# A new order of the expert products on TensorE, with gathers issued further ahead and gate weights freed by their own semaphore

## The chip, the cores and the metric

The kernel runs on one core of one Trainium2 chip. The metric is the device time of one execution in microseconds (us), the median of several runs. The profile is one execution of its own, taken by the hardware profiler; its times within the program are counted from the start of the span.

## The reference, cut to what matters

One layer of an encoder runs over 576 tokens (512 of a prompt, 64 of a running stream): a projection, two state-space mixers, cross-attention, and a mixture of experts at the end. The change lies in the last part alone. Each token picks one group of experts and two experts in it; the sum runs over 32 experts.

```python
for e in range(N_EXPERTS):          # 32 experts, d_model 1024, hidden width 256
    hid = silu(t @ w_gate[e]) * (t @ w_up[e])
    out = out + (hid @ w_down[e]) * combine[:, e:e + 1]
```

Each of w_gate, w_up and w_down of one expert has 1024 x 256 float32 numbers, 1 MB. All 32 experts together are 96 MB of weights that are read from HBM once.

## The kernel before, in words

The kernel is written engine by engine, with every wait on a semaphore by hand. There is no scheduler: the order on each engine is the order of the code.

**Routing.** After the attention a table of slots gives each expert up to 80 tokens (CAP). The normed token rows lie in HBM (`ffn_rows`); results go to `expert_rows` in HBM and are mixed at the very end, after all experts.

**One expert n on TensorE (PE).** Four steps, each with its own line: `turn_x` (L1385) transposes the gathered rows `xg` in 8 small matmuls (all transposes carry the helper's line L907); `gate_up` (L1393) makes the gate product and then the up product, 32 matmuls each (all carry L1407, and the trace records them as 64); `down_rows` (L1411) makes the down product in 24 matmuls (L1423, recorded as 48). In the loop of `pe_pass` (L1429) the order is: transposes of n, down product of n-1, gate product of n, up product of n.

**The other compute engines.** ScalarE (ACT) copies half of the transposed rows to `xgT` (L1758), applies silu to the gate product (L1763) and copies part of the down product to `yo` (L1771, L1772). VectorE (DVE) copies the other half (L2306), multiplies silu(gate) by up into `hid` (recorded at the helper's line L1816) and copies the rest of the down product (L2319, L2320). All of these have two buffers, one for even and one for odd experts.

**Weights.** There are five sets of three weight buffers (gate, up, down; `WSET`). The loads of experts 0 to 4, 15 transfers, are issued before the expert stage, as buffers of earlier stages come free. From then on `reload` (L678) on SyncE (SP) fills a buffer again when it is free, one transfer of 1 MB (L675) each, always in the order gate, up, down: expert 31 into the set of expert 0, then expert 5 into the set of expert 1, and so on to expert 30 into that of expert 26. The waits stand in this order on the one SP queue:

```python
if part < 2:
    sp.wait_ge(gu_done, N + 1)        # gate and up: up product of the old expert done
else:
    sp.wait_ge(dn_done, 2 * N + 2)    # down: its down product done
load_part(BODY * i + n, set_of(n), part)
```

So SP asks for no gate weights of the next expert before the down weights of this one have been asked for.

**Rows.** GpSimd (POOL) gathers the rows of an expert from `ffn_rows` into one of two `xg` buffers (`gather`, L840, issued at L851) and scatters `yo` to `expert_rows` (`scatter`, L856, issued at L866), both as indirect DMAs. In `pool_pass` (L871) it issues the gather of expert n+2 and then the scatter of expert n.

**After the experts.** When all scatters have landed SP loads `expert_rows` (L728) and the final norm follows. In between SP issues one load of the final norm's gain (L591), right behind the last weights.

Of the kernel before, what the change touches and what calls it, by code (L numbers as in the profile page):

```python
# [216 lines left out]
def build(nc, a, o):  # L217
# [14 lines left out]
    with ExitStack() as ctx:  # L232
# [346 lines left out]
        def _(sp):  # L579
# [162 lines left out]
        def _(pool):  # L742
# [97 lines left out]
            def gather(pp, i, b, reused=True):  # L840

                if reused:
                    pool.wait_ge(turned_x, 4 * pp + (2 * b - 2))
                    pool.sem_inc(waits_done, 1)
                    pool.tensor_copy(cur_x[0:CAP, b:b + 1], idx_x[0:CAP, bass.ds(2 * i + b, 1)]).then_inc(gx_copied, 1)  # L845
                    pool.wait_ge(gx_copied, 2 * pp + (b - 1))
                    pool.sem_inc(waits_done, 1)
                    rows_now = cur_x[0:CAP, b:b + 1]
                else:
                    rows_now = idx_x[0:CAP, b:b + 1]  # L850
# [5 lines left out]
            def scatter(pp, i, b, reused=True):  # L856

                if reused:
                    pool.wait_ge(scattered[b], 16 * pp)
                    pool.sem_inc(waits_done, 1)  # L860
                pool.tensor_copy(cur_y[0:CAP, b:b + 1], idx_y[0:CAP, bass.ds(2 * i + b, 1)]).then_inc(gy_copied, 1)
                pool.wait_ge(gy_copied, 2 * pp + (b + 1))
                pool.wait_ge(yo_act, 2 * pp + (b + 2))
                pool.wait_ge(yo_dve, 2 * pp + (b + 2))
                pool.sem_inc(waits_done, 1)
                pool.indirect_dma_start(  # L866
                    out=y2_dram[:, :], out_offset=bass.IndirectOffsetOnAxis(ap=cur_y[0:CAP, b:b + 1], axis=0),
                    in_=yo[b][0:CAP], in_offset=None,
                    bounds_check=2 * T - 1, oob_is_err=False).then_inc(scattered[b], 16)

            def pool_pass(p):  # L871
                first = p * (LAST + 1)
# [12 lines left out]
                for b in range(2):  # L885
                    scatter(first + LAST, LAST, b)
                for b in range(2):
                    pool.wait_ge(scattered[b], 16 * (first + LAST + 1))
                pool.sem_inc(pass_done, 1)
# [6 lines left out]
        def _(pe):  # L896
# [488 lines left out]
            def turn_x(pp, b):  # L1385

                pe.wait_ge(gathered[b], 16 * pp + 16)
# [5 lines left out]
            def gate_up(N, n, i, p, reused=True):  # L1393

                s, b = set_of(n), n % 2
                gate, up = [w.rearrange("p (k n) -> p k n", k=KD) for w in WSET[s][0:2]]
# [4 lines left out]
                for part, (w, done) in enumerate(((gate, gate_done), (up, gu_done))):  # L1401
                    wait_expert_chunk(pe, part, n, i, p)
                    for j in range(2):
                        for k in range(KD):
                            for half in range(2):
                                cols = slice(HD * half, HD * (half + 1))
                                m = pe.matmul(banks[2 + part][cols, CAP * j:CAP * (j + 1)], w[:, k, j::2][:, cols],  # L1407
                                              xgT[b][:, k, :], start=(k == 0), stop=(k == KD - 1))
                    m.then_inc(done, 1)
# [19 lines left out]
            def pe_pass(p):  # L1429
# [14 lines left out]
                turns = (NE - 4) // BODY  # L1444
                with pe.Fori(0, turns) as i:
# [29 lines left out]
        def _(act):  # L1475
# [279 lines left out]
            def copy_x(pp, b):  # L1755

                act.wait_ge(turned_x, 4 * pp + (2 * b + 1))
# [3 lines left out]
            def act_expert(pp, b, last=False, reused=True):  # L1761
                act.wait_ge(gate_done, 2 * pp + (b + 1))
                act.activation(gact[b].rearrange("p j l -> p (j l)"), banks[2][:, 0:2 * CAP], ACT.Silu)\  # L1763
                    .then_inc(silu_done, 1)
                if not last:
                    copy_x(pp + b, 1 - b)
                act.wait_ge(dn_done, 4 * pp + (2 * b + 1))
                if reused:
                    act.wait_ge(scattered[b], 16 * pp)
# [4 lines left out]
            def act_pass(p):  # L1774
                first = p * (LAST + 1)
                again = not isinstance(p, int)
                copy_x(first, 0)
                for b in range(2):
                    act_expert(first, b, reused=again)
                with act.Fori(1, LAST) as i:  # L1780
                    for b in range(2):
                        act_expert(first + i, b)
                for b in range(2):
                    act_expert(first + LAST, b, last=(b == 1))
# [15 lines left out]
        def _(dve):  # L1800
# [502 lines left out]
            def copy_x(pp, b):  # L2303

                dve.wait_ge(turned_x, 4 * pp + (2 * b + 2))
# [3 lines left out]
            def dve_expert(pp, b, last=False, reused=True):  # L2309
                dve.wait_ge(silu_done, 2 * pp + (b + 1))  # L2310
                dve.wait_ge(gu_done, 2 * pp + (b + 1))
                tt(hid[b].rearrange("p j l -> p (j l)"), gact[b].rearrange("p j l -> p (j l)"),
                   banks[3][:, 0:2 * CAP]).then_inc(hid_ready, 1)
                if not last:
                    copy_x(pp + b, 1 - b)
                dve.wait_ge(dn_done, 4 * pp + (2 * b + 2))
                if reused:
                    dve.wait_ge(scattered[b], 16 * pp)
# [25 lines left out]
            def dve_pass(p):  # L2344
# [24 lines left out]
                copy_x(first, 0)  # L2369
                for b in range(2):  # L2370
                    dve_expert(first, b, reused=again)
                with dve.Fori(1, LAST) as i:
                    for b in range(2):
                        dve_expert(first + i, b)
                for b in range(2):
                    dve_expert(first + LAST, b, last=(b == 1))
# [55 lines left out]
```

## Time and profile before

| what | value |
|---|---|
| runs before | 908.38, 908.22, 906.3 us; median 908.22 us |
| the profiled execution's own time | 909.06 us |
| its span in the profile | 907.3 us, so 1.76 us lie around it |
| mean granted TensorE clock | 0.966 of full speed |
| TensorE busy, share of the span | 91% (weight loads 75%) |
| VectorE, ScalarE, GpSimd busy | 39%, 23%, 15% |
| bytes moved by DMA | 167.61 MB, mean 185 GB/s |
| the expert stage, first transposes to last down product | 581.7 to 869.0 us of the span |

A busy TensorE in this profile is not a TensorE at its peak, since matmuls are pipelined. In the views, PE is TensorE's matmuls, PEld its weight loads. "DMA share" is the mean busy share of the core's 16 DMA engines, and every wait on a transfer counts 16 arrivals. An entry in brackets at the end of a row of the timeline is the idle time of that engine before the row and what ended it.

### The profile page before, as it was taken

The page shows a single profiled execution, that of the slowest core. Times are in us where ns is not written, and L with a number is a line of the kernel's source. Part 1 is how long each engine was busy: PE and PEld are TensorE (multiplying, and loading weights), DVE is VectorE, ACT ScalarE, POOL GpSimd, SP SyncE. Part 2 cuts the span into 40 slices and gives each one's busy share as a digit, 9 for nine tenths or more (in the row PEclk, how much of TensorE's full clock was granted, in tenths as well). Part 3 has the DMA queues.
Part 4 walks back from the last instruction along what each step waited for, and adds up shares of the span by engine and source line. Part 5 has one row for each costly group of instructions (what it writes and reads, how often), then busy time and mean ns, then how long its engine had stood idle before and what let it go on. Part 6 is the DMA issues. An engine that isn't in the chain of part 4 may idle for free. (4 is left out here: it accounts for less than half of the span.)

```text
span 907.3 us, 21592 instructions
## 1 busy us (share of the span) xinstructions
PE 829.5 (91%) x9261; PEld 682.2 (75%) x9261; DVE 350.1 (39%) x791; ACT 211.5 (23%) x484; POOL 136.1 (15%) x173
## 2 busy tenths in 40 slices
PE   3999999899999999999999998699999999998925
PEld 2777877677888888877888886578788788777722
DVE  5599987425551123401223447411211211111216
ACT  2302206425221201112221212122222222221203
POOL 1191100004420000000000000123232232222100
PEclk9999999989999999999999998599999999999977
DMA  9742174102121850151022324589999999999335
GB/s 239 230 112 42 21 173 139 47 12 96 47 94 70 292 184 1 61 172 47 1 92 71 135 98 183 232 317 374 376 373 383 372 394 371 382 363 331 127 113 224
DMA packets 76535, 167.61 MB, mean 185 GB/s; under 512 B 25712, under 2 KB 56560, under 8 KB 63616
## 3 DMA queue, kind: packets, MB, share of 16 engines
q1 hardware_dynamic: 61060, 151.45, 46.8%
q0 software_dynamic: 6144, 9.45, 3.1%
q10 hardware_dynamic: 9276, 5.93, 2.2%
q8 instruction: 40, 0.66, 0.3%
q14 instruction: 15, 0.12, 0.0%
HBM read 158.09 MB, written 17.88 MB: 194 GB/s over the span
## 5 line engine op out<-in xcount | busy, mean ns | idle before, releaser
L940 PE MATMUL bank<-act_a,weight_ring 128*128 128x288 f32 x768 | 192.2, 412 | 3.4 <-ACT act_a L1487 1.8
L940 PEld LDWEIGHTS bank<-act_a,weight_ring 128*128 128x128 f32 x768 | 146.9, 193 | 44.5 <-ACT act_a L1487 2.4
L1229 PE MATMUL bank<-weight_ring,act_b 128*128 128x256 f32 x512 | 111.8, 379 | 0.0
L1229 PEld LDWEIGHTS bank<-weight_ring,act_b 128*128 128x128 f32 x512 | 96.7, 190 | 12.9
L1816 DVE TENSOR_TENSOR region_t<-region_t,bank 128x160 f32<-128x160 f32 (+3 forms) x47 | 15.5, 331 | 147.6 <-PE bank L1407 147.1
L1407 PE MATMUL bank<-region_t,weight_ring 128*64 128x80 f32 x1536 | 58.4, 235 | 4.7 <-DMA weight_ring<-in_w_up 4.0
L1407 PEld LDWEIGHTS bank<-region_t,weight_ring 128*64 128x64 f32 x1536 | 55.8, 140 | 8.6 <-DMA weight_ring<-in_w_up 4.6
L866 POOL DMA_INDIRECT expert_rows<-region_r,scatter_now x32 | 30.1, 941 | 191.0 <-DVE region_r L2320 191.0
L1130 PE MATMUL bank<-weight_ring,region_u 128*128 128x256 f32 x256 | 56.6, 380 | 0.0
L1130 PEld LDWEIGHTS bank<-weight_ring,region_u 128*128 128x128 f32 x256 | 48.4, 190 | 6.5
L1816 DVE TENSOR_TENSOR region_u<-region_u,bank 128x512 f32<-128x512 f32 (+1 forms) x26 | 17.8, 686 | 90.2 <-PE bank L1229 66.1
L1487 ACT ACTIVATE act_a<-bank 128x512 f32<-128x512 f32 (+1 forms) x46 | 22.5, 523 | 118.2 <-PE bank L907 91.1
L907 PE MATMUL bank<-ident,region_r 80*128 80x80 f32 (+1 forms) x324 | 45.0, 282 | 3.8 <-DMA region_r<-ffn_rows,gather_index 3.8
L907 PEld LDWEIGHTS bank<-ident,region_r 80*128 80x128 f32 (+1 forms) x324 | 39.0, 191 | 8.1 <-issue 3.9
L2319 DVE COPY region_r<-bank 16x256 f32<-16x256 f32 x32 | 13.7, 429 | 78.3 <-PE bank L1423 78.3
L834 POOL MEMSET region_r<- 80x1024 f32 x2 | 1.8, 948 | 262.4 <-PE bank L1298 262.4
L1407 PEld LDWEIGHTS bank<-region_t,region_g 128*64 128x64 f32 x1024 | 36.8, 138 | 5.2 <-issue 3.0
L1407 PE MATMUL bank<-region_t,region_g 128*64 128x80 f32 x1024 | 39.0, 234 | 1.5 <-DMA region_g<-in_w_up 1.5
L1771 ACT ACTIVATE region_r<-bank 32x256 f32<-32x256 f32 x64 | 24.2, 378 | 67.3 <-PE bank L1423 66.9
L907 PE MATMUL bank<-ident,row_stage 128*128 128x128 f32 (+2 forms) x141 | 20.4, 295 | 18.9 <-DVE row_stage L1834 17.0
L907 PEld LDWEIGHTS bank<-ident,row_stage 128*128 128x128 f32 (+2 forms) x141 | 17.1, 158 | 22.1 <-issue 18.4
L851 POOL DMA_INDIRECT region_r<-ffn_rows,gather_now x30 | 29.3, 976 | 25.9 <-POOL gather_now L845 14.7
(341 smaller groups left out, 1146.5 us busy)
## 6 DMA issues: line engine op xcount, KB each, us to landing
weight_ring<-in_w_up SPq DMA_DIRECT2D x17, 1024.0 KB
weight_ring<-in_w_down SPq DMA_DIRECT2D x10, 1024.0 KB, 6.3
weight_ring<-in_w_in SPq DMA_DIRECT2D x8, 1024.0 KB, 7.6
region_g<-in_w_up SPq DMA_DIRECT2D x8, 1024.0 KB
region_g<-in_w_gate SPq DMA_DIRECT2D x8, 1024.0 KB
conv_io<-in_w_gate SPq DMA_DIRECT2D x8, 1024.0 KB
conv_io<-in_w_down SPq DMA_DIRECT2D x8, 1024.0 KB
weight_ring<-in_w_gate SPq DMA_DIRECT2D x7, 1024.0 KB
```

The costliest lines, as they stand in the source:

```text
L834: pool.memset(xg[b][0:CAP], 0.0).then_inc(xg_zero, 1)
L851: pool.indirect_dma_start(out=xg[b][0:CAP], out_offset=None, in_=xf_dram[:, :], in_offset=bass.IndirectOffsetOnAxis(ap=rows_now, axis=0), ...
L866: pool.indirect_dma_start(out=y2_dram[:, :], out_offset=bass.IndirectOffsetOnAxis(ap=cur_y[0:CAP, b:b + 1], axis=0), in_=yo[b][0:CAP], in_ ...
L907: return pe.transpose(out, in_, ident[0:m, 0:m])
L940: m = pe.matmul(ps[:, 0:HALF], slot(c)[:, k, P * (mt % 2):P * (mt % 2 + 1)], x[:, k, HALF * h:HALF * (h + 1)], start=(k == 0), stop=(k == ...
L1130: m = pe.matmul(ps[:, 0:CW], mnT[:, k, P * t:P * (t + 1)], slot(first_chunk + c)[:, k, :], start=(k == 0), stop=(k == KD - 1))
L1229: m = pe.matmul(ps[0:L, CW * cc:CW * (cc + 1)], x[:, k, t0:t0 + L], slot(c)[:, k, :], start=(k == 0), stop=(k == KD - 1))
L1407: m = pe.matmul(banks[2 + part][cols, CAP * j:CAP * (j + 1)], w[:, k, j::2][:, cols], xgT[b][:, k, :], start=(k == 0), stop=(k == KD - 1))
L1487: act.activation(dst, src, func, scale=scale).then_inc(emptied["act"], 1)
L1771: act.activation(yo[b][DB * blk:DB * (blk + 1), 3 * CW:D], down_block(b, blk, 3), ACT.Copy)
L1816: return dve.tensor_tensor(out, x, y, op)
L2319: dve.tensor_copy(yo[b][DB * 2:CAP, 3 * CW:D], down_block(b, 2, 3))
```

## The change

TensorE's order per expert becomes: gate product of n, transposes of n+1, down product of n-1, up product of n. `gate_up` is split into `gate` and `up` over one helper `hidden`. The gate product now waits for the silu of the expert before (`silu_done`) where `gate_up` waited for its `hid_ready`. On SP the load into a gate buffer waits for `gate_done` instead of `gu_done`; the order gate, up, down on the queue stays. On POOL the first four gathers are issued ahead of everything else as their buffers come free, and then gather n+4 stands before scatter n; there are still two `xg` buffers, so gather N waits until expert N-2 has been transposed, as before. ACT and DVE follow the new order. Counts of instructions, transfers and bytes stay the same.

```diff
                 for part in range(3):
-                    if part < 2:
+                    if part == 0:
+                        sp.wait_ge(gate_done, N + 1)
+                    elif part == 1:
                         sp.wait_ge(gu_done, N + 1)
                     else:
                         sp.wait_ge(dn_done, 2 * N + 2)
...
-            def gather(pp, i, b, reused=True):
+            def gather(n, i, p, reused=True):
+                b, N = n % 2, NE * p + 2 * i + n
                 if reused:
-                    pool.wait_ge(turned_x, 4 * pp + (2 * b - 2))
+                    pool.wait_ge(turned_x, 2 * (N - 1))
...
+                for n in range(4):
+                    gather(n, 0, p, reused=n >= 2)
+                for n in range(2):
+                    gather(n + 4, 0, p)
+                    scatter(n, 0, p, reused=again)
+                with pool.Fori(0, (NE - 6) // 2) as i:
+                    for n in range(2, 4):
+                        gather(n + 4, i, p)
+                        scatter(n, i, p)
+                for n in range(NE - 4, NE):
+                    scatter(n, 0, p)
                 for b in range(2):
-                    gather(first, 0, b, reused=again)
-                for b in range(2):
-                    gather(first + 1, 1, b)
-                    scatter(first, 0, b, reused=again)
-                with pool.Fori(1, LAST) as i:
-                    for b in range(2):
-                        gather(first + i + 1, i + 1, b)
-                        scatter(first + i, i, b)
...
+            def gate(N, n, i, p, reused=True):
                 pe.wait_ge(xT_act, N + 1)
                 pe.wait_ge(xT_dve, N + 1)
                 if reused:
-                    pe.wait_ge(hid_ready, N)
+                    pe.wait_ge(silu_done, N)
+                hidden(0, gate_done, n, i, p)
+            def up(n, i, p):
+                hidden(1, gu_done, n, i, p)
...
-                turn_x(N0 // 2 if not again else p * (NE // 2), 0)
-                gate_up(N0, 0, 0, p, reused=again)
-                turn_x(p * (NE // 2), 1)
+                turn_x(0, 0, p)
+                gate(N0, 0, 0, p, reused=again)
+                turn_x(1, 0, p)
+                up(0, 0, p)
+                gate(N0 + 1, 1, 0, p)
+                turn_x(2, 0, p)
                 down_rows(N0, 0, 0, p, reused=again)
-                gate_up(N0 + 1, 1, 0, p)
+                up(1, 0, p)
...
                     for n in range(2, 2 + BODY):
-                        turn_x(p * (NE // 2) + i * (BODY // 2) + n // 2, n % 2)
+                        gate(N0 + i * BODY + n, n, i, p)
+                        turn_x(n + 1, i, p)
                         if n == 2:
                             down_rows(N0 + i * BODY + 1, BODY + 1, i - 1, p)
                         else:
                             down_rows(N0 + i * BODY + (n - 1), n - 1, i, p)
-                        gate_up(N0 + i * BODY + n, n, i, p)
+                        up(n, i, p)
                 for n in range(NE - 2, NE):
-                    turn_x(p * (NE // 2) + n // 2, n % 2)
+                    gate(N0 + n, n, 0, p)
+                    if n < NE - 1:
+                        turn_x(n + 1, 0, p)
                     down_rows(N0 + n - 1, n - 1, 0, p)
-                    gate_up(N0 + n, n, 0, p)
+                    up(n, 0, p)
                 down_rows(N0 + NE - 1, NE - 1, 0, p)
...
                 with act.Fori(0, (NE - 4) // 2) as i:
                     for n in range(3, 5):
                         act_gate(n, i, p)
                         copy_x(n + 1, i, p)
                         act_rows(n - 1, i, p)
...
                 with dve.Fori(0, (NE - 4) // 2) as i:
                     for n in range(3, 5):
                         copy_x(n + 1, i, p)
                         dve_rows(n - 1, i, p)
                         dve_hidden(n, i, p)
```

## Rows read from the trace of the kernel before

**Rows 1.** Page, part 2: DMA share in 40 slices of the span.

```profile
DMA  9742174102121850151022324589999999999335
```

**Rows 2.** Waits of TensorE's matmuls, 560 to 870 us: total us, times, longest.

```profile
PE bank L1407 <- DMA weight_ring<-in_w_up: 4.0, 4, 1.3
PE bank L907 <- DMA region_r<-ffn_rows,gather_index: 3.8, 1, 3.8
...
PE bank L1423 <- DVE region_t L1816: 2.8, 7, 0.5
PE bank L1407 <- DMA act_a<-in_w_up: 1.8, 2, 1.2
PE bank L1407 <- DMA region_g<-in_w_up: 1.5, 2, 1.0
```

**Rows 3.** Timeline of TensorE, one expert in the middle (start us, us, instructions).

```profile
694.89 1.11 PE L907 MATMUL bank<-ident,region_r 80*128 80x80 f32 x8
695.93 2.80 PE L1423 MATMUL bank<-act_a,region_t 128*32 128x256 f32 x48
698.66 2.44 PE L1407 MATMUL bank<-region_t,conv_io 128*64 128x80 f32 x64
700.93 2.44 PE L1407 MATMUL bank<-region_t,region_g 128*64 128x80 f32 x64
```

**Rows 4.** Timeline of TensorE, first and last wait for up weights, and the end.

```profile
788.41 2.44 PE L1407 MATMUL bank<-region_t,weight_ring 128*64 128x80 f32 x64 [1.27 <-DMA weight_ring<-in_w_up]
...
854.90 2.44 PE L1407 MATMUL bank<-region_t,weight_ring 128*64 128x80 f32 x64 [0.53 <-DMA weight_ring<-in_w_up]
857.27 1.11 PE L907 MATMUL bank<-ident,region_r 80*128 80x80 f32 x8
858.31 2.80 PE L1423 MATMUL bank<-weight_ring,region_t 128*32 128x256 f32 x48
861.04 2.44 PE L1407 MATMUL bank<-region_t 128*64 128x80 f32 x64
863.31 2.38 PE L1407 MATMUL bank<-region_t,weight_ring 128*64 128x80 f32 x64
866.18 2.80 PE L1423 MATMUL bank<-weight_ring,region_t 128*32 128x256 f32 x48 [0.49 <-DVE region_t L1816]
```

**Rows 5.** Windows: us, busy PE PEld DVE ACT POOL, granted clock, DMA share, GB/s.

```profile
580.00:590.00 10.00, 7.65 (x116) 7.47 (x118) 1.27 (x3) 2.02 (x3) 2.36 (x4) 0.54 0.07 20
590.00:600.00 10.00, 10.00 (x218) 8.43 (x214) 1.66 (x4) 2.09 (x5) 2.32 (x4) 1.00 0.80 302
...
620.00:780.00 160.00, 157.76 (x3450) 130.59 (x3440) 30.64 (x74) 39.32 (x94) 42.80 (x74) 1.00 1.00 380
...
830.00:860.00 30.00, 27.71 (x586) 21.90 (x589) 5.48 (x13) 6.50 (x16) 5.76 (x10) 1.00 0.49 179
```

**Rows 6.** Page, part 6: the load behind the last weights, us from issue to landing.

```profile
gain_rows<-in_norm_final SPq DMA_DIRECT2D x1, 512.0 KB, 32.2
```

**Rows 7.** Timeline of all engines, the first expert, with SP's issues.

```profile
583.65 4.54 PE L1407 MATMUL bank<-region_t 128*64 128x80 f32 x64 [0.63 <-ACT region_t L1758]
...
587.94 2.97 PE L1407 MATMUL bank<-region_t,weight_ring 128*64 128x80 f32 x64
...
590.84 1.11 PE L907 MATMUL bank<-ident,region_r 80*128 80x80 f32 x8
590.93 0.33 SPq L675 DMA_DIRECT2D region_t<-in_w_gate  x1
...
591.31 0.43 SPq L675 DMA_DIRECT2D weight_ring<-in_w_up  x1
...
594.74 0.33 SPq L675 DMA_DIRECT2D weight_ring<-in_w_down  x1
...
600.14 0.35 SPq L675 DMA_DIRECT2D conv_io<-in_w_gate  x1
```

**Rows 8.** Page, part 3: GpSimd's queue of gathers and scatters, share of 16 engines.

```profile
q0 software_dynamic: 6144, 9.45, 3.1%
```

More of the change, by code:

```diff
@@ L849, in gather @@
                 else:
-                    rows_now = idx_x[0:CAP, b:b + 1]
+                    rows_now = idx_x[0:CAP, n:n + 1]
                 pool.indirect_dma_start(
@@ L854, in gather, with scatter @@
                     bounds_check=T - 1, oob_is_err=False).then_inc(gathered[b], 16)
-            def scatter(pp, i, b, reused=True):
+            def scatter(n, i, p, reused=True):
+                b, N = n % 2, NE * p + 2 * i + n
                 if reused:
-                    pool.wait_ge(scattered[b], 16 * pp)
+                    pool.wait_ge(scattered[b], 16 * (NE // 2) * p + 16 * i + 16 * (n // 2))
                     pool.sem_inc(waits_done, 1)
[L861 to L864, printed above, removed]
+                pool.tensor_copy(cur_y[0:CAP, b:b + 1], idx_y[0:CAP, bass.ds(2 * i + n, 1)]).then_inc(gy_copied, 1)
+                pool.wait_ge(gy_copied, N + 1)
+                pool.wait_ge(yo_act, N + 2)
+                pool.wait_ge(yo_dve, N + 2)
                 pool.sem_inc(waits_done, 1)
@@ L871, in pool_pass @@
             def pool_pass(p):
-                first = p * (LAST + 1)
                 again = not isinstance(p, int)
@@ L875, in pool_pass @@
                 pool.sem_inc(waits_done, 1)
-                for b in range(2):
-                    gather(first, 0, b, reused=again)
-                for b in range(2):
-                    gather(first + 1, 1, b)
-                    scatter(first, 0, b, reused=again)
-                with pool.Fori(1, LAST) as i:
-                    for b in range(2):
-                        gather(first + i + 1, i + 1, b)
-                        scatter(first + i, i, b)
[L885 to L888, printed above, removed]
+                for n in range(4):
[9 more added lines that the diff above has]
+                    scatter(n, 0, p)
+                for b in range(2):
+                    pool.wait_ge(scattered[b], 16 * (NE // 2) * p + 16 * (NE // 2))
                 pool.sem_inc(pass_done, 1)
@@ L1383, in _, with turn_x @@
                 pe.wait_ge(emptied[who], count[who])
-            def turn_x(pp, b):
-                pe.wait_ge(gathered[b], 16 * pp + 16)
+            def turn_x(n, i, p):
+                b = n % 2
+                pe.wait_ge(gathered[b], 16 * (NE // 2) * p + 16 * (BODY // 2) * i + 16 * (n // 2 + 1))
                 for h in range(2):
@@ L1391, in turn_x, with hidden @@
                     m.then_inc(turned_x, 1)
-            def gate_up(N, n, i, p, reused=True):
+            def hidden(part, done, n, i, p):
                 s, b = set_of(n), n % 2
-                gate, up = [w.rearrange("p (k n) -> p k n", k=KD) for w in WSET[s][0:2]]
+                w = WSET[s][part].rearrange("p (k n) -> p k n", k=KD)
+                wait_expert_chunk(pe, part, n, i, p)
+                for j in range(2):
+                    for k in range(KD):
+                        for half in range(2):
+                            cols = slice(HD * half, HD * (half + 1))
+                            m = pe.matmul(banks[2 + part][cols, CAP * j:CAP * (j + 1)], w[:, k, j::2][:, cols],
+                                          xgT[b][:, k, :], start=(k == 0), stop=(k == KD - 1))
+                m.then_inc(done, 1)
+            def gate(N, n, i, p, reused=True):
                 pe.wait_ge(xT_act, N + 1)
@@ L1399, in gate_up @@
                 if reused:
-                    pe.wait_ge(hid_ready, N)
[L1401 to L1409, printed above, removed]
+                    pe.wait_ge(silu_done, N)
+                hidden(0, gate_done, n, i, p)
+            def up(n, i, p):
+                hidden(1, gu_done, n, i, p)
             def down_rows(N, n, i, p, reused=True):
@@ L1438, in pe_pass @@
                 pe.wait_ge(idx_ready, p + 1)
[L1439 to L1441 removed]
+                turn_x(0, 0, p)
[4 more added lines that the diff above has]
+                turn_x(2, 0, p)
                 down_rows(N0, 0, 0, p, reused=again)
[L1443 to L1445 removed]
+                up(1, 0, p)
+                with pe.Fori(0, (NE - 4) // BODY) as i:
                     for n in range(2, 2 + BODY):
[L1447 removed]
+                        gate(N0 + i * BODY + n, n, i, p)
+                        turn_x(n + 1, i, p)
                         if n == 2:
@@ L1774, in act_pass @@
             def act_pass(p):
-                first = p * (LAST + 1)
                 again = not isinstance(p, int)
[L1777 to L1784, printed above, removed]
+                copy_x(0, 0, p)
+                act_gate(0, 0, p)
+                copy_x(1, 0, p)
+                for n in range(1, 3):
+                    act_gate(n, 0, p)
+                    copy_x(n + 1, 0, p)
+                    act_rows(n - 1, 0, p, reused=again)
+                with act.Fori(0, (NE - 4) // 2) as i:
+                    for n in range(3, 5):
+                        act_gate(n, i, p)
+                        copy_x(n + 1, i, p)
+                        act_rows(n - 1, i, p)
+                act_gate(NE - 1, 0, p)
+                act_rows(NE - 2, 0, p)
+                act_rows(NE - 1, 0, p)
             act.sem_inc(yo_act, 1)
@@ L2368, in dve_pass @@
                     expert_gates()
[L2369 to L2376, printed above, removed]
+                copy_x(0, 0, p)
+                copy_x(1, 0, p)
+                dve_hidden(0, 0, p)
+                for n in range(1, 3):
+                    copy_x(n + 1, 0, p)
+                    dve_rows(n - 1, 0, p, reused=again)
+                    dve_hidden(n, 0, p)
+                with dve.Fori(0, (NE - 4) // 2) as i:
+                    for n in range(3, 5):
+                        copy_x(n + 1, i, p)
+                        dve_rows(n - 1, i, p)
+                        dve_hidden(n, i, p)
+                dve_rows(NE - 2, 0, p)
+                dve_hidden(NE - 1, 0, p)
+                dve_rows(NE - 1, 0, p)
             dve.sem_inc(yo_dve, 1)
```

42 lines of the change are left out of this document (23 added, 19 removed).

## The prediction

> **What bounds the kernel now.** I read the DMA line of the page first, because the change touches only the expert stage and that stage moves 96 MB of weights. From about two thirds of the span on, the 16 DMA engines are 90% busy or more for ten slices of 22.7 us each [rows 1]. The reader is to see that this is the expert stage, and that it begins with a hole: from 580 to 590 us the share is 0.07, then 0.80, and from 620 to 780 us it is 1.00 at 380 GB/s [rows 5].
>
> Next I read what TensorE waits for. In a middle expert its steps follow one another without a gap: transposes 1.04 us (695.93 less 694.89), down product 2.73, gate product 2.27 [rows 3], up product 2.37 (857.27 less 854.90) [rows 4]. That is 8.41 us of work per expert. Its waits on the way are small: 2.8 us for VectorE's `hid`, and 4.0 + 1.8 + 1.5 = 7.3 us for up weights; for gathered rows it waits once, 3.8 us before expert 0 [rows 2]. Taken alone this would say that TensorE is the bound.
>
> The last two views say otherwise. The waits for up weights are eight, one per expert, and all late: the first such up product starts at 788.41 us, the last at 854.90 [rows 4]: 66.49 / 7 = 9.50 us per expert, 1.1 us more than PE's work. So in the end PE follows the transfers, one per 9.50 / 3 = 3.17 us. And not all DMA engines are equal: from 830 to 860 us the mean share is only 0.49 [rows 5], while PE is still waiting for up weights at 854.90 [rows 4] and the gain's load right behind the last weights takes 32.2 us to land [rows 6]. Some engines have long finished and a few have not; a transfer counts when its last part is there. **The bound is the slowest DMA engine**, which works through 81 transfers from SP's first issue at 590.93 us [rows 7] to the end: to 854.90 it has done 80 of them, (854.90 - 590.93) / 80 = 3.30 us each, close to the 3.17 at which PE visibly waits for it. There is no room for much idle time in between. So the end of the stage is: when this engine starts, plus its fixed work, plus what PE must still do after the last weights.
>
> **The change, part by part.**
>
> *Volume.* 81 transfers, 32 gathers, 32 scatters before and after: 0.
>
> *PE's steadier order.* The gaps for `hid` (2.8 us in all [rows 2]) go, since a gate product and transposes now lie between the up product and the down product that needs `hid`. With 8.41 us per expert against 9.50 PE only waits longer for weights: 0 on the path. The copies and products on ACT and DVE change places too; with ACT busy 39.32 and DVE 30.64 of 160 us [rows 5] they are hidden, and if that cover went, a late `xgT` copy would hold the next gate product.
>
> *The start.* Gate product 0 ends where the up product starts, at 587.94 us; up ends at 590.84 and SP issues 0.09 later [rows 7]. The first transfer (expert 31's gate) moves from 590.93 to 588.03, **2.90 us earlier**. But then SP stands at its second and third wait, and these come later in PE's new order. After gate 0 come transposes of 1 (to 589.1, a little long at the low clock), up 0 (2.37, to 591.5), gate 1 (2.27), transposes of 2 (1.04), down 0 (2.73, to 597.5). So the up transfer is issued at 591.6 instead of 591.31 and the down transfer at 597.6 instead of 594.74 [rows 7]; expert 5's gate load, free since 593.8, stands behind that down wait on SP and goes out with it, instead of at 600.14. Before, three transfers from 590.93 at 3.17 us last to 600.4, just when the fourth is issued at 600.14 [rows 7]: no gap. After, the third starts at 597.6 and ends at 600.8, the fourth ends at 603.9 against 603.6 before: 0.3 us later. In the new gap, however, the engine does the rows of one more gather, since POOL no longer issues gathers behind a scatter. All gathers and scatters take 3.1% of 16 engines' span [rows 8], 28.1 us per engine, 0.44 us per transfer spread evenly, 0.88 if half of the engines carry it. Bounds of the term: -2.9 (the whole lead is kept) to +0.4. I take +0.3 - 0.88 = **-0.6 us**, with the uneven value, because the engines visibly end unevenly [rows 5, 6].
>
> *Later releases.* In every later round the down weights are asked for 2.27 us later and the gate weights 2.37 us earlier than before, as seen from the up product. The queue of the slowest engine is never empty then (1.1 us of arrears are added per expert), and its order is still gate, up, down: 0. If the arrears were not there, each round would lose up to 2.3 us.
>
> *Gathers.* POOL's wait for transposes n+2 now stands ahead of scatter n. These transposes come before down product n on PE, so the scatter queued behind that wait is not delayed by it. A gather still has two experts' time to land, and PE never waits for one in the stage's course [rows 2]: 0.
>
> *The tail.* This is the part that I expect to cost. Before, PE waits for the last up weights; from the start of up 30 at 854.90 to the start of the last down product at 866.18 are 11.28 us [rows 4]: up, transposes, down, gate, up and 0.49 of wait. After, PE meets expert 30's gate weights first. They land one transfer before the up weights, and behind them stand gate 30 (2.27), transposes 31 (1.04), down 29 (2.73), up 30 (2.37), gate 31 (2.27), down 30 (2.73), up 31 (2.38), wait (0.49): 16.28 us. From the landing of the up weights that is 16.28 - 3.17 = 13.11, so **+1.8 us**. The up and down weights of 30 land meanwhile. Bounds: 0, if PE no longer has to wait at gate 30, to 16.28 - 2.76 - 11.28 = +2.2, with a transfer spacing of 1.05 MB at the middle stretch's 380 GB/s [rows 5]. PE is ready for gate 30 only some 8.4 us after it began gate 29, against 9.5 between landings, so I take the value near the upper end.
>
> *Sum.* -0.6 + 1.8 = +1.2 us on the profiled execution's own 909.06 us (span 907.3 and 1.76 around it), 910.3 us. That execution lies 0.84 us above the median of the runs, 908.22; the same step from the median gives **909.4 us**. The bounds add up to -2.9 and +2.6, or 905.3 to 910.8. Before's three runs spread over 2.1 us; a change under 0.3% (2.7 us) can't be told from none.
>
> **The rivals.**
>
> *A. The earlier first transfer is kept.* The slowest engine would then do useful work from 588.03 on without a gap and everything ends 2.9 us earlier; with the tail, -2.9 + 1.8 = -1.1, 907.1 us. For it: the hole from 580 to 590 us [rows 5]. Against it: SP's order on the queue. The Trainium skill, "DMA: Bandwidth & Descriptors", section "Rules for kernel authors", advises to issue a DMA early, compute, and wait late. By that rule this lead is the gain; the trace of before shows only that the first transfer waits for the up product.
>
> *B. PE becomes the pace.* If the weights keep up with 8.41 us per expert, the wait for up weights is gone and gate 31 starts at 591.5 + 30 x 8.41 = 843.8; then 2.27 + 2.73 + 2.38 + 0.49 bring the last down product to 851.7 instead of 866.18: -14.5, 893.7 us, or half of it if only part of the waits goes. For it: PE's 157.76 busy of 160 us in the middle [rows 5]. Against it: 9.50 us per expert as soon as the early stock of weights is used up [rows 4].
>
> *C. TensorE's clock rises later.* It was granted 0.54 of full speed from 580 to 590 us and 1.00 from 590 to 600 [rows 5]; before it rose, PE ran gate 0 and the beginning of up 0. The new order puts eight short transposes into that place. If the low level (1.2 instead of 2.4 GHz) lasts until up 0 has ended, up 0 costs what gate 0 did, 4.29 us instead of 2.27 [rows 7, 4], some 2.0 more, and with it every release behind it, at a moment at which the DMA engines are idle: +1.2 + 2.0 = +3.2, 911.4 us, slower. It decides from the point at which the clock has not risen by 591.5 us. For it: the transposes have short streams. Against it: they follow without a gap. The skill's "TensorE: Matmul & The Clock Gate", section "What's actually happening", says that the number of slow matmuls at the start differs between runs of one kernel; no run here shows that.
>
> *D. The change doesn't do what it says.* "Gate weights first" holds for one transfer alone; from then on the gate load stands behind the down wait. This is part of the forecast, not a case of its own.
>
> **How the numbers follow.** The forecast, 909.4 us, gets 0.58; of that 0.15 lies above +2.7 us, by the upper bounds and the runs' spread. A gets 0.10 (no change that can be told), B 0.17 (faster), C 0.12 (slower), anything else 0.03 (slower). Faster by over 0.3%: 0.17. Within 0.3%: 0.43 + 0.10 = 0.53. Slower: 0.15 + 0.12 + 0.03 = 0.30. The range goes from the forecast's lower bound, 905.3, rounded to 905.0, to beyond C, 912.0; B and the 0.03 are left out.
>
> **What would show it.** Right: the first SP issue of the stage at 588, the third near 597.6 with the fourth right behind it; PE's waits for up weights gone and as large or larger ones for gate weights from about the same expert on, 9.5 us apart; the last wait of this kind about three microseconds before 854.9; the last down product near 867. Wrong: no waits for weights at all and the last down product before 860 (B); a first transfer followed by a busy DMA share and the last down product before 866 (A); a granted clock that rises only after 591.5 us (C); or waits for gathers on PE.

## The result, and the profile after

The changed kernel takes **914.25 us** (median of 10 executions, 909.44 to 918.74), the kernel before, run beside it, 907.92: ratio **1.0063, 95% interval 1.0037 to 1.0089**. It is slower by over 0.3%, and above the forecast range of 905.0 to 912.0. The profiled execution (span 907.7, own time 909.44) is the fastest of its ten, so its trace shows what the change does to the waits, but not the whole loss.

What PE waits for, from 560 to 880 us (columns as in [rows 2]):

```profile
PE bank L1406 <- DMA region_g<-in_w_gate: 4.2, 3, 2.8
...
PE bank L910 <- DMA region_r<-ffn_rows,gather_index: 3.9, 1, 3.9
PE bank L1406 <- DMA act_b<-in_w_gate: 3.7, 2, 2.1
PE bank L1406 <- DMA weight_ring<-in_w_gate: 3.7, 3, 2.7
...
PE bank L1406 <- DMA conv_io<-in_w_gate: 1.3, 2, 1.1
...
PE bank L1434 <- DVE region_t L1843: 0.5, 1, 0.5
```

As forecast, the waits for up weights are gone and waits for gate weights stand in their place. There are ten, 12.9 us in all, against eight of 7.3 us before, and they begin sooner: the first at 742.93 us, against 788.41 for the first up product that waited [rows 4]. The waits for `hid` fell from 2.8 to 0.5 us, and that bought nothing, because PE now arrives earlier at weights that come no earlier. PE's timeline, the first wait, the two longest, the last one and the end, against [rows 4]:

```profile
742.93 2.44 PE L1406 MATMUL bank<-region_t,weight_ring 128*64 128x80 f32 x64 [0.30 <-DMA weight_ring<-in_w_gate]
...
782.85 4.00 PE L1406 MATMUL bank<-region_t,weight_ring 128*64 128x80 f32 x64 [2.68 <-DMA weight_ring<-in_w_gate]
...
812.63 2.44 PE L1406 MATMUL bank<-region_t,region_g 128*64 128x80 f32 x64 [2.82 <-DMA region_g<-in_w_gate]
...
851.26 2.44 PE L1406 MATMUL bank<-region_t,region_g 128*64 128x80 f32 x64 [0.44 <-DMA region_g<-in_w_gate]
...
867.64 2.80 PE L1434 MATMUL bank<-weight_ring,region_t 128*32 128x256 f32 x48 [0.49 <-DVE region_t L1843]
```

The last down product starts at 867.64, forecast "near 867". The reader is also to see the second row: that gate product took 4.00 us instead of 2.44. From 783.5 to 786.9 us the granted clock was 0.50, the 1.2 GHz level, right after 2.68 us of waiting. SP's queue in the first rounds, against [rows 7]:

```profile
588.08 0.33 SPq L675 DMA_DIRECT2D region_t<-in_w_gate  x1
591.61 0.33 SPq L675 DMA_DIRECT2D weight_ring<-in_w_up  x1
597.62 0.33 SPq L675 DMA_DIRECT2D weight_ring<-in_w_down  x1
598.32 0.35 SPq L675 DMA_DIRECT2D conv_io<-in_w_gate  x1
599.96 0.34 SPq L675 DMA_DIRECT2D region_g<-in_w_up  x1
605.97 0.33 SPq L675 DMA_DIRECT2D conv_io<-in_w_down  x1
```

The first load goes out 2.85 us earlier than in [rows 7], the third 2.88 us later: SP stands 6.0 us at the wait for the down product. Then three loads go out within 2.3 us (597.62 to 599.96), and again nothing for 6.0. The windows (columns as in [rows 5]):

```profile
580.00:590.00 10.00, 7.80 (x104) 7.36 (x106) 1.50 (x3) 2.46 (x4) 2.08 (x4) 0.55 0.16 37
590.00:600.00 10.00, 10.00 (x238) 8.52 (x236) 1.66 (x4) 2.09 (x5) 2.83 (x5) 1.00 0.70 251
620.00:780.00 160.00, 156.78 (x3424) 127.75 (x3416) 31.18 (x75) 38.94 (x93) 42.99 (x76) 1.00 1.01 382
780.00:830.00 50.00, 43.76 (x916) 35.79 (x914) 8.31 (x20) 10.45 (x25) 11.20 (x20) 0.97 0.97 354
830.00:860.00 30.00, 26.42 (x578) 21.53 (x576) 5.03 (x13) 6.26 (x15) 5.19 (x9) 1.00 0.46 169
```

What the DMA engines gain before 590 us (share 0.16 for 0.07) they lose from 590 to 600 (0.70 for 0.80). From 830 to 860 the mean share is 0.46 while PE still waits at 851.26: so the load that PE waits for still ends later than most of the engines' work.

### The profile page after: what moved, and what is told of

It reads as the page before. It is cut to its first block and busy times, and to the rows that moved or that the text cites. A ratio compares the mean times of both kernels' runs of the same rounds, so it can differ in the third digit from the quotient of the medians.

```text
span 907.7 us, 21617 instructions
## 1 busy us (share of the span) xinstructions
PE 828.4 (91%) x9261; PEld 680.7 (75%) x9261; DVE 350.2 (39%) x791; ACT 211.3 (23%) x484; POOL 135.6 (15%) x173
## 2 busy tenths in 40 slices
DMA packets 76535, 167.61 MB, mean 185 GB/s; under 512 B 25712, under 2 KB 56560, under 8 KB 63616
## 5 line engine op out<-in xcount | busy, mean ns | idle before, releaser
L1232 PEld LDWEIGHTS bank<-weight_ring,act_b 128*128 128x128 f32 x512 | 96.8, 190 | 12.9
L2334 DVE COPY region_t<-bank 128x320 f32<-128x320 f32 x32 | 15.7, 491 | 111.6 <-PE bank L910 111.6
L1782 ACT ACTIVATE region_t<-bank 128x160 f32<-128x160 f32 x32 | 9.7, 303 | 146.6 <-PE bank L1406 146.6
```

The costliest lines, as they stand in the source:

```text
L1232: m = pe.matmul(ps[0:L, CW * cc:CW * (cc + 1)], x[:, k, t0:t0 + L], slot(c)[:, k, :], start=(k == 0), stop=(k == KD - 1))
```

## The experiments

Theory: the slowest DMA engines set the pace, and the change costs because SP's queue (gate, up, down) no longer has the order in which PE uses the weights (gate of n+1, down of n, up of n+1). Rivals: the early gate load itself costs (e2, e10, e13, e14), or the clock that falls behind long waits (e6, e9). The expectations call this last one "theory 2" in e1 to e6 and "theory C" in e9 and e11; it is not rival C of the prediction, which was about the start of the stage. The table gives all seventeen runs. "Stage" is worked out from the trace: start of the last down product less start of the first transposes.

| run | kernel | median us | ratio, 95% | stage us |
|---|---|---|---|---|
| | before, first trace | 907.92 | | 284.46 |
| e5 | before again, one execution | 903.93 | | 281.04 |
| | changed, first trace | 914.25 | 1.0063, 1.0037 to 1.0089 | 286.07 |
| e1 | changed again | 913.15 | 1.0045, 1.0023 to 1.0068 | 285.28 |
| e11 | changed, third time | 913.17 | 1.0060, 1.0037 to 1.0083 | 286.84 |
| e2 | changed, gate freed with up | 910.87 | 1.0022, 0.9999 to 1.0044 | 287.07 |
| e10 | the same again | 910.89 | 1.0027, 1.0004 to 1.0050 | 284.16 |
| e13 | changed, only first gate load early | 910.68 | 1.0032, 1.0012 to 1.0052 | 282.68 |
| e14 | changed, only later gate loads early | 916.45 | 1.0100, 1.0078 to 1.0121 | 287.09 |
| e6 | changed, eight spare products | 921.13 | 1.0143, 1.0119 to 1.0167 | 294.95 |
| e9 | changed, three spare products | 912.52 | 1.0054, 1.0032 to 1.0076 | 285.19 |
| e3 | changed, loads in order of use | 905.73 | 0.9952, 0.9934 to 0.9971 | 277.78 |
| e15 | the same, three loads together | 904.71 | 0.9968, 0.9951 to 0.9986 | 279.23 |
| e4 | before, gate freed first | 904.68 | 0.9951, 0.9933 to 0.9969 | 276.93 |
| e7 | before, rows spread | 896.91 | 0.9873, 0.9850 to 0.9896 | 269.98 |
| e8 | changed, rows spread | 893.92 | 0.9853, 0.9825 to 0.9882 | 268.42 |
| e12 | order of use, rows spread | 896.04 | 0.9866, 0.9841 to 0.9891 | 269.26 |
| e16 | before, gate freed first, rows spread | 896.35 | 0.9872, 0.9848 to 0.9896 | 269.65 |
| e17 | changed, gate freed with up, rows spread | 897.41 | 0.9852, 0.9827 to 0.9878 | 269.65 |

The runs of before beside them had medians of 907.3 to 910.2 us.

### How far single executions differ (e1, e5, e11)

No edit.

> The changed kernel once more, unchanged. Its ten runs lie between 909.44 and 918.74 us (median 914.25), the profiled one is the fastest of them. Theory 1 (order of use): gate weights are needed before the down weights but are loaded behind them, so TensorE waits longer and more unevenly, and the last weights leave more products behind them; then this execution shows waits for gate weights of 15 us or more in all and the last down product at 868 to 876 us. Theory 2 (clock): a wait for gate weights of some 2.7 us or more lowers the granted clock, as once at 782 us in the first profile, where one gate product took 4.00 instead of 2.27 us; then this execution has several stretches under full clock between 740 and 870 us, and its excess over 909 us is about their extra time. Theory 3 (transfers): the weights themselves land later; then the last wait for gate weights ends later than 851.3 us by as much as the time is longer, with no lower clock.

> The kernel before once more, for a second trace of it. Two traces of the changed kernel had an expert stage (start of the first transposes to start of the last down product) of 286.07 and 285.28 us against 284.46 in the one trace of before, yet the medians differ by 4 to 6 us. If the stage of before is usually shorter than in its one trace, this one is at 280 to 283 us; if the difference lies elsewhere, it is at 284 to 285 again.

> The changed kernel unchanged, a third time, beside the two above on the same chip: ratio 1.0045 to 1.0063, and at least one stretch at half clock between 740 and 860 us, behind a wait for gate weights of over 2.3 us, if theory C holds; a trace with no such stretch at this ratio speaks against it.

The loss holds in all three comparisons of the changed kernel. The trace of e1 has nine waits for gate weights, 11.9 us in all where theory 1 had asked for 15 or more, and two gate products behind waits of 2.66 and 2.40 us took 3.89 and 4.01 us. But executions of one kernel differ by several microseconds in stages that the change doesn't touch. PE's first product in the first projection and the first transposes of the expert stage, in the first trace of the changed kernel:

```profile
22.84 5.55 PE L943 MATMUL bank<-act_a,weight_ring 128*128 128x288 f32 x16 [1.32 <-ACT act_a L1503]
...
581.57 1.31 PE L910 MATMUL bank<-ident,region_r 80*128 80x80 f32 x8 [3.93 <-DMA region_r<-ffn_rows,gather_index]
```

and in e1:

```profile
22.84 7.00 PE L943 MATMUL bank<-act_a,weight_ring 128*128 128x288 f32 x16 [1.32 <-ACT act_a L1503]
...
587.19 1.31 PE L910 MATMUL bank<-ident,region_r 80*128 80x80 f32 x8 [3.97 <-DMA region_r<-ffn_rows,gather_index]
```

Same code, same start, 1.45 us more for the first product; the expert stage begins 5.62 us later; where the rest of that comes from is not shown. Before's own stage was 284.46 us in the first trace and 281.04 in e5. So a median carries an unknown mix of early and late starts, and a difference of 2 or 3 us between two kernels is read beside the stage's length in their traces. By the stages the change costs 286.1 (mean of three) less 282.8 (mean of two), 3.3 us, of the 4 to 6 that the medians show; the two traces of before are themselves 3.4 us apart, so this is rough.

### What the early gate load is worth (e2, e10, e13, e14, e4)

In e2 and e10 SP waits for the up product again before it loads gate weights; all else is the changed kernel:

```diff
-                    if part == 0:
-                        sp.wait_ge(gate_done, N + 1)
-                    elif part == 1:
+                    if part < 2:
                         sp.wait_ge(gu_done, N + 1)
```

In e13 the early wait is kept for the first load alone, in e14 for all others alone. In e4 the kernel before gets the early wait and nothing else.

> The changed kernel with the gate load waiting for the up product again, as before; TensorE's new order stays. Theory 1: the loads still arrive in the order gate, up, down, so the time stays near the changed kernel's 914 us (912 to 917); the first transfer of the stage is issued near 591.6 instead of 588.1 us. If freeing the gate buffer first were what costs, it would come back to 908. Theory 2: as theory 1, since the waits for gate weights stay.

> The changed kernel with the gate weights freed by the end of the up product once more, for a second pair with the changed kernel. If the order of PE alone costs what the tail was priced at, 909.5 plus 1.8, ratio 1.002; if the first try was a lucky one, 1.0045 to 1.0063 like the changed kernel.

> The changed kernel, the gate weights freed early for the first load alone, then by the up product. If the loss sits in the later loads (issued three at a time), 910 to 911.5, ratio 1.002, like the kernel with no early release; if the first load does the harm, 913.3, ratio 1.005.

> The changed kernel, the first gate load freed by the up product and all later ones early. If the loss sits in the later loads, 913.3, ratio 1.005; if in the first one, 910 to 911.5, ratio 1.002.

> The kernel before with only the gate buffer freed by the gate product. Load order and order of use agree there. Theory 1: the lead of up to 2.9 us of the first transfer is worth something because nothing else moves: 905 to 908 us, not slower than before. If early release of gate weights as such were the harm, it would be slower than 910.

PE's new order alone costs 0.22% and 0.27%, 2.0 and 2.5 us, with intervals that begin at nothing. With the early release the median is 913.3 us (31 executions of the changed kernel) against 910.9 (24 of e2 and e10): means 2.5 us apart, with 1.0 to 3.9 as the 95% interval. The fastest and the slowest executions shift alike, 909.44 to 919.22 against 906.50 to 915.56, so a different share of late starts does not account for it alone. The release, forecast as a small gain, is a small loss here by the times. The stages can't confirm it: 286.1 us against 285.6 (mean of e2 and e10, which are 2.9 apart).

On the first load alone it costs nothing (910.68), and the traced execution of e13 has a stage of 282.68 us, shorter than all of e2, e10, e14 and the changed kernel. On the later loads alone it is 916.45, against 913.3 expected. That run's traced execution began its stage at 586.70, though, and its stage, 287.09 us, is no longer than the one of e2: how much of its 5.6 us belongs to the release is not settled. Together the two runs point to the later loads, and not to the first.

In the old order the same release gains 0.49%. SP's queue of e4 shows the difference:

```profile
588.41 0.33 SPq L675 DMA_DIRECT2D region_t<-in_w_gate  x1
591.08 0.33 SPq L675 DMA_DIRECT2D weight_ring<-in_w_up  x1
594.88 0.33 SPq L675 DMA_DIRECT2D weight_ring<-in_w_down  x1
597.38 0.35 SPq L675 DMA_DIRECT2D conv_io<-in_w_gate  x1
599.44 0.34 SPq L675 DMA_DIRECT2D region_g<-in_w_up  x1
```

One load every two to four microseconds, since PE gives the buffers free in the order in which SP waits for them. From 590 to 600 us the DMA share is 0.90:

```profile
590.00:600.00 10.00, 10.00 (x221) 8.43 (x217) 1.99 (x5) 2.09 (x5) 2.32 (x4) 1.00 0.90 342
```

The first load leads by 2.5 us (588.41 for 590.93), and the stage is 276.93 us against 284.46 and 281.04. That is more than the lead; where the rest comes from is not shown.

### The loads in the order of use (e3, e15)

```diff
+                def round_(i, n):
+                    reload(p, i, n, n - BODY, 0)
+                    reload(p, i, n - 1, n - 1 - BODY, 2)
+                    reload(p, i, n, n - BODY, 1)
```

In a round SP asks for the gate weights of this expert, the down weights of the one before and the up weights of this one. e15 is e3, but from the sixth expert loaded on the gate load waits for its up product too.

> The changed kernel with one edit on SyncE's queue: the loads are asked for in TensorE's new order of use, gate of the next expert, down of this one, up of the next. Theory 1: the waits become short and even again, the last weights leave less work behind them (10.2 us from the start of up 30 to the last down product instead of 16.3 from gate 30), and the time falls to 905 to 908 us, 6 us or more under the changed kernel. Theory 2: the same if the waits stay under 2 us each, and no stretch under full clock after 590 us. Theory 3: the stream of transfers is as long as in the changed kernel, so the time stays at 912 or more.

> Loads in order of use, but from the sixth expert loaded on each gate load waits for its up product, so that three loads are issued within 1 us and then none for 7; the first loads go out as before. If three at a time costs by itself, 908 to 910 (2.4 us or more over 905.73); if only start and order count, 905 to 906.5.

With the queue in PE's order the changed kernel is faster than before, and some 8 us faster than with the old queue (913.15 to 905.73 on the same chip, 7.4; the stage falls from 286.1 to 277.78, 8.3). SP's queue of e3, whose stage began at 585.24:

```profile
590.85 0.33 SPq L675 DMA_DIRECT2D region_t<-in_w_gate  x1
594.27 0.33 SPq L675 DMA_DIRECT2D weight_ring<-in_w_up  x1
596.49 0.33 SPq L675 DMA_DIRECT2D conv_io<-in_w_gate  x1
600.28 0.33 SPq L675 DMA_DIRECT2D weight_ring<-in_w_down  x1
602.63 0.33 SPq L675 DMA_DIRECT2D region_g<-in_w_up  x1
```

The third load goes out 11.25 us after the stage began (12.28 in e15); in the changed kernel it is 16.05 (597.62 less 581.57). And at the end the gate weights no longer stand behind down weights that are used after them. How the 8 us divide between the denser start and the order of landing is not separated: e3 and e15 have both. e15 rules out that three loads in a row cost by themselves, in this order of loads. Its queue in the middle:

```profile
652.06 0.33 SPq L675 DMA_DIRECT2D weight_ring<-in_w_gate  x1
652.59 0.33 SPq L675 DMA_DIRECT2D weight_ring<-in_w_down  x1
653.02 0.38 SPq L675 DMA_DIRECT2D weight_ring<-in_w_up  x1
660.41 0.33 SPq L675 DMA_DIRECT2D act_b<-in_w_gate  x1
```

7.4 us without a load, yet 904.71 us.

### Does the low clock cost? (e6, e9)

Both add spare 128x128 products on PE, whose results nobody reads, ahead of the gate's wait for weights, experts 18 to 29: eight in e6 (`fill`), three in e9.

```diff
+                for _ in range(fill):
+                    pe.matmul(banks[2][:, 256:384], ident[:, :], ident[:, :], start=True, stop=True)
```

> The changed kernel with eight spare 128x128 matmuls (about 1.1 us, into unused columns of the gate bank) ahead of the wait for gate weights, from expert 18 to 29. Theory 2 (clock): the idle times ahead of gate products become shorter by that, none is over 2 us, the granted clock stays at full speed from 590 us to the end of the stage, and the time falls by 1 to 3 us to 910 to 912. Theory 1 (order of use): the transfers set the pace, so the spare work is hidden and the time stays within 1.5 us of the changed kernel's 913 to 914; nothing is gained by a steadier clock.

> The changed kernel with three spare 128x128 products (0.77 us by the last try, where eight took 2.05 us) ahead of the wait for the gate weights, experts 18 to 29; PE's work then stays near 9.4 us an expert, under the pace of the loads. Theory C (the half clock after a wait of over 2.4 us is what separates the changed kernel from the one with its gate weights freed with the up weights): no granted clock under 1.0 from 600 to 860 us, and 1.5 to 3 us off the changed kernel, ratio about 1.002. Rival (the clock is a side show): the same time as the changed kernel, 1.0045 to 1.0063, with the clock steady.

e6 was sized wrongly: eight of them took 2.05 us, not the 1.1 I had reckoned with, and at 8.4 + 2.05 us per expert PE became the bound: no waits for weights, 921.13 us. It says nothing about the clock. e9 does. Its weight waits and its window from 780 to 830:

```profile
PE bank L1406 <- DMA region_g<-in_w_gate: 2.1, 2, 1.7
...
PE bank L1406 <- DMA act_b<-in_w_gate: 1.3, 1, 1.3
...
PE bank L1406 <- DMA conv_io<-in_w_gate: 0.2, 1, 0.2
```

```profile
780.00:830.00 50.00, 48.33 (x973) 39.42 (x975) 8.80 (x21) 10.90 (x26) 11.70 (x21) 1.00 0.98 361
```

The clock stays at 1.00, from 600 us to the end of the stage too. The waits fall from 12.9 to 3.6 us, about what the spare products take: 12 times 0.87 us from their start to the gate product's (the expectation had 0.77), 10.4 us. And the time stays where it was: 1.0054, where theory C asked for about 1.002. While the transfers set the pace, a slow product between two waits shows no cost. So the half clock does not explain the loss.

### Even out the DMA engines (e7, e8, e12, e16, e17)

An expert has fewer rows than its 80 slots (576 tokens x 2 / 32 = 36 on average), and they fill the slots from the first. The edit puts slot a + 16b on partition 5a + b, so that the same rows are gathered and scattered by partitions all over the 80:

```diff
-                step(dve.tensor_copy(slot_id, iot[:, 0:CAP]))
+                step(dve.tensor_copy(slot_id.rearrange("p (a b) -> p a b", b=5),
+                                     iot[:, 0:CAP].rearrange("p (b a) -> p a b", a=16)))
```

> The kernel before with one edit on VectorE: the slot numbers are laid out so that the tokens of an expert fall on every fifth partition first (partition 5a+b holds slot a+16b) instead of on the first 30 to 45 of 80 partitions. Bytes, rows and instructions stay. Theory of the slowest DMA engine: rows of gathers and scatters have so far fallen on the same engines for every expert; spread evenly, all engines end together, the weights come at about PE's own pace of 8.6 us per expert and the time falls by 6 to 10 us, to 899 to 903. If all engines were equally loaded already, nothing changes (908 to 910).

> The changed kernel with the same even spread of rows. If the slowest DMA engine is what makes the new order wait, the waits for gate weights nearly vanish, PE runs at 8.4 us per expert and this kernel is as fast as or faster than the spread kernel with the old order: 895 to 902 us. If the new order costs something of its own (clock, copies), it stays 4 us or more above it.

> Loads in the order of use, with the rows spread over the DMA engines. If the order of the loads only mattered because one engine ran late, nothing is left of its 8 us: 893 to 895, as the changed kernel with its rows spread (893.92). If it is worth something on its own, 886 to 890.

> The kernel before with the gate weights freed first and the rows spread. If the slowest DMA engine was all that the early release helped, 896 to 897 (as the kernel before with its rows spread, 896.91); if the earlier stream is worth something by itself, 892 to 894.

> The changed kernel with the gate weights freed by the up product and the rows spread. If the early release only costs while one engine runs late, the same as the changed kernel with its rows spread, 893 to 895; if it costs by itself, 2.4 us or more less, 889 to 891.5.

All five lie between 893.92 and 897.41 us, and no trace of them has a wait for weights. Windows of e7 (before, spread):

```profile
620.00:780.00 160.00, 159.33 (x3508) 130.86 (x3506) 31.57 (x76) 39.70 (x95) 44.19 (x77) 1.00 1.01 394
...
830.00:860.00 30.00, 28.52 (x620) 22.51 (x616) 6.15 (x15) 7.62 (x18) 5.65 (x10) 1.00 0.29 100
```

and of e8 (changed, spread):

```profile
620.00:780.00 160.00, 160.00 (x3512) 131.09 (x3504) 31.59 (x76) 39.74 (x95) 43.74 (x77) 1.00 1.02 393
...
830.00:860.00 30.00, 22.44 (x504) 17.08 (x496) 4.85 (x12) 6.45 (x15) 4.27 (x7) 0.93 0.19 64
```

The engines move 393 GB/s instead of 382 in the middle, and they end closer together: the gain's load behind the last weights lands 19.0 us after its issue (e8) instead of 29.5. The share of the last stretch falls from 0.46 to 0.19, in part because the stage of e8 ends 17.5 us earlier. The row work itself did not shrink; the queue of gathers and scatters on the page of e8, against [rows 8]:

```profile
q0 software_dynamic: 6144, 9.45, 3.3%
```

So it is the spread that counts. The traces show the mean of the 16 engines and not each one, so how many ran late stays open. The stage is 268.4 to 270.0 us in all five, whatever the order of the products, of the loads and of the releases. So everything that tells the orders apart, the change's loss included, shows only while some engines run late. Against what was expected, e7 and e8 came 2.1 and 1.1 us below their ranges, e12 and e17 1.0 and 2.4 above. These versions are the best of the study; e8, the changed kernel, has the lowest median, but between the five the intervals decide nothing.

## Why the prediction was wrong

**The bound** was right: DMA engines that run late, shown by the spread rows; that it is one engine is not shown. **Volume, PE's steadier order and the gathers**, all 0, fit the runs: both traces have 76535 packets and 167.61 MB, the `hid` waits went without a gain, and PE waits for a gather once, 3.9 us before expert 0, as in [rows 2].

**The start** was right in its course. I named issues at 588.03, 591.6 and 597.6 us with the fourth right behind; they came at 588.08, 591.61, 597.62 and 598.32. Its value of -0.6 leaned on row work done in the gap; the medians of e13 against e2 and e10 show no gain, within about 2 us, while the stage in e13's trace is 1.5 and 4.4 us shorter than in theirs. The term stays unmeasured.

**The tail** was right: from the last wait's end at 851.26 to the last down product at 867.64 are 16.38 us, forecast 16.28, and the order alone (e2, e10) costs 2.0 and 2.5 us where I had +1.8. Two signs were off, though: the waits begin four experts sooner than before and not at about the same one (gate 19 at 742.93, up 23 at 788.41, counted back from expert 30), and they lie on average (851.26 - 742.93) / 11 = 9.85 us apart, not 9.5.

**The step that failed** is "Later releases": "The queue of the slowest engine is never empty then (1.1 us of arrears are added per expert), and its order is still gate, up, down: 0." Unchanged, the order was no longer that of PE. In its place the runs show a price of some 8 us for the old queue under the new order (e3, e15 against the changed kernel), of which the tail term held 1.8. And they show that the early release, a gain of 0.49% under the old order, is worth nothing or less under the new one: +2.5 us by the means, where start and later releases together stood at -0.6. With the 2.0 to 2.5 of the order alone this makes 4.5 to 5 of the 4 to 6 us measured. The first half of the step held: the DMA share from 620 to 780 us is 1.01. Why the later early releases cost at all is not settled. e9 speaks against the half clock, e15 against three loads in a row (in the other order of loads), and with even engines nothing is left of it (e8, e17); a part of it may be the mix of late starts.

**The range** failed with it. It allowed for a spread of 2.1 us seen in three runs; the ten of the changed kernel spread over 9.3, and the starts of the stage in two of its traces are 5.6 us apart. The profiled execution alone, 909.44 us against a forecast of 910.3 for it, would have looked like a hit. It is the fastest of the ten, so that is luck.

**The rivals.** A (the lead is kept) did not come; SP's order was the reason given, and the third load did go out 2.88 us later. e4 is that rival with PE's old order, and there it holds. The Trainium skill, "DMA: Bandwidth & Descriptors", section "Rules for kernel authors", advises to issue early and wait late; e4 agrees (0.9951). In the changed kernel, where SP stood 6.0 us at the next wait but one, the same early issue brought nothing. B (PE the pace) came only with the spread rows, 8.4 us per expert. C: the clock rose in time at the start, 1.00 from 590 us in the first trace; it fell later, with no price that e9 shows. D was part of the forecast and was right.

## What to carry to other kernels

A queue of loads has an order, and it should be the order in which the consumer uses the data; who reorders the consumer reorders the loads with it, or may pay while the loads set the pace, here some 8 us. An early release helped here where the next waits on the same queue came soon after it (e4), and not where the queue then stood. And before the order of a transfer-bound stage is tuned, see whether the DMA engines end together: here one line that spreads the rows gave 1.3 to 1.5%, more than any order.

## What the runs showed of the hardware

The granted clock fell to 0.50 in the middle of a dense stage (783.5 to 786.9 us in the changed kernel), behind a wait of 2.68 us; the wait of 2.82 us at 812.63 in the same trace was followed by a product at full speed (2.44 us). In e10 it fell behind a wait of 2.09 us, in e13 it did not behind one of 2.51 (2.44 us). The length of the wait alone doesn't decide it.

The first product of the first projection took 5.55 us in one execution and 7.00 in another, with the same start at 22.84. The Trainium skill, "TensorE: Matmul & The Clock Gate", section "What's actually happening", says that the number of slow matmuls at the start differs between runs of one kernel; the lengths of these two rows agree. The granted clock of both traces reads 1.00 from 22 to 30 us, so no view here shows the low level itself.
